# Grouped-query attention in a two-layer block: one more step between scores and transposes, with the dense products as a stage of their own

## The reference, cut to what matters

```python
qa, ka, va, za, qb, kb, vb, zb, ga, gb = split_cols(jnp.einsum('bld,de->ble', rms_norm_2(x, norm_g), w_in))
qa = apply_axial_rope(rms_norm_2(qa, q_norm_g), cos, sin)      # ka likewise
s = jnp.einsum('bqkgd,bskd->bkgqs', qb, k) * HEAD_DIM ** -0.5  # gqa_attention, 8 heads on 2 key heads
p = jax.nn.softmax(s, axis=-1)
oa = jnp.einsum('bkgqs,bskd->bqkgd', p, v) * jax.nn.silu(za)
```

## Time and profile before

| | |
|---|---|
| runs | 1706.32, 1709.43, 1713.77 us |
| profiled execution | 1706.15 us, span 1704.8 us, mean TensorE clock 0.982 |
| busy in the span | PE 1621.7 us (95%), DVE 872.2 (51%), ACT 620.7 (36%) |
| grouped attention of layer 0 | about 783.7 to 916 us of the span |
| grouped attention of layer 1 | about 1278 to 1422.5 us of the span |

### The profile page before, as it was taken

How to read it: one execution, slowest core, us unless ns; L and a number is a source line. 1 busy time by engine, 2 the same in 40 slices (tenths; PEclk the granted TensorE clock), 3 DMA queues, 4 the chain that set the end, 5 groups by cost and what they waited for, 6 DMA issues and landing times.

```text
span 1704.8 us, 24772 instructions
## 1 busy us (share of the span) xinstructions
PE 1621.7 (95%) x10349; PEld 1381.2 (81%) x10349; DVE 872.2 (51%) x1560; ACT 620.7 (36%) x1100; POOL 52.4 (3%) x52
## 2 busy tenths in 40 slices
PE   7999989999999999999999898999999998989997
PEld 5898767777888888899888777999988877667886
DVE  4434555556644655945554454346554455444543
ACT  5232244344322333723344342223233343433233
POOL 0000000000000000020000000000020000000000
PEclk9999989999999999999999899999999999999999
DMA  6234400014333322422111201224422112012331
GB/s 192 75 78 93 105 13 13 26 57 121 93 99 99 99 99 75 112 50 75 50 51 30 71 26 63 76 86 137 75 51 74 50 50 68 20 38 85 101 111 50
DMA packets 175599, 125.21 MB, mean 73 GB/s; under 512 B 48752, under 2 KB 172272, under 8 KB 175488
## 3 DMA queue, kind: packets, MB, share of 16 engines
q1 hardware_dynamic: 175488, 123.63, 25.4%
HBM read 121.52 MB, written 2.10 MB: 73 GB/s over the span
## 4 chain that ended last, share of the span: by engine, by line
PE 89%; DVE 4%; ACT 3%; issue 2%; POOL 0%; DVEq 0%; ACTq 0%; POOLq 0%
PE bank L576 69%; PE bank L2648 2%; PE bank L2680 2%; PE bank L2660 2%; PE bank L1581 2%; PE bank L3028 1%; PE bank L1540 1%; PE bank L2559 1%; PE bank L2991 1%; ACT w_hi L523 1%; PE bank L1467 1%; PE bank L1242 1%; PE bank L2510 1%; PE bank L3007 1%; ACT probs L1520 1%
## 5 line engine op out<-in xcount | busy, mean ns | idle before, releaser
L576 PE MATMUL bank<-h_hi,w_hi 128*128 128x512 f32 (+2 forms) x920 | 326.8, 375 | 9.4 <-issue 4.1
L532 DVE TENSOR_TENSOR w_lo<-w_raw,w_hi 128x2048 fp32r<-128x2048 f32 (+2 forms) x117 | 241.2, 2061 | 183.2 <-ACT w_hi L523 182.9
L576 PE MATMUL bank<-h_lo,w_hi 128*128 128x512 f32 (+2 forms) x920 | 322.4, 370 | 0.0
L576 PE MATMUL bank<-h_hi,w_lo 128*128 128x512 f32 (+2 forms) x920 | 320.9, 369 | 0.0
L523 ACT ACTIVATE w_hi<-w_raw 128x2048 fp32r<-128x2048 f32 (+2 forms) x117 | 201.1, 1720 | 67.0 <-DMA w_raw<-w_in 30.4
L576 PEld LDWEIGHTS bank<-h_hi,w_hi 128*128 128x128 f32 (+1 forms) x920 | 166.4, 189 | 53.0 <-issue 19.2
L576 PE MATMUL bank<-g_hi,w_hi 128*128 128x264 f32 (+1 forms) x784 | 197.8, 316 | 3.2 <-DVE g_lo L1693 1.8
L576 PE MATMUL bank<-g_lo,w_hi 128*128 128x264 f32 (+1 forms) x784 | 195.0, 312 | 0.0
L576 PE MATMUL bank<-g_hi,w_lo 128*128 128x264 f32 (+1 forms) x784 | 194.3, 311 | 0.0
L576 PEld LDWEIGHTS bank<-h_hi,w_lo 128*128 128x128 f32 (+1 forms) x920 | 166.5, 189 | 30.6
L576 PEld LDWEIGHTS bank<-h_lo,w_hi 128*128 128x128 f32 (+1 forms) x920 | 166.2, 189 | 29.5 <-issue 0.5
(11 more groups left out here) (561 smaller groups left out, 2578.4 us busy)
## 6 DMA issues: line engine op xcount, KB each, us to landing
w_raw<-w_in SPq DMA_DIRECT2D x45, 1024.0 KB, 5.3
w_raw<-w_up SPq DMA_DIRECT2D x32, 512.0 KB, 4.9
w_raw<-w_in SPq DMA_DIRECT2D x40, 256.0 KB, 4.5
w_raw<-w_down SPq DMA_DIRECT2D x8, 1024.0 KB, 5.1
w_raw<-w_out SPq DMA_DIRECT2D x8, 1024.0 KB, 5.1
w_raw<-w_out SPq DMA_DIRECT2D x8, 512.0 KB, 3.4
w_raw<-w_ple_gate SPq DMA_DIRECT2D x4, 1024.0 KB, 5.1
w_raw<-w_o_attn SPq DMA_DIRECT2D x8, 512.0 KB, 3.4
```

The lines of the kernel that those rows point to most:

```text
L532: DV.e.tensor_tensor(wlo[u % RING][:, 0:n], raw[u % RING][:, 0:n], whi[u % RING][:, 0:n].bitcast(F32), ALU.subtract).then_inc(*w_low(u))
L576: ins = PE.e.matmul(out, stationary[a](k), moving[b](k)[i], start=first and n == 0, stop=last and n == 2)
```

## The change

`filled` already has a parameter `apart`. With it, `pipeline` gets the stages score, give, turn, value, so that step s of the schedule is: score of item s, fill of item s - 1, turn of item s - 2, value of item s - 3. The change sets it in the three streams of the grouped attention, for both layers. No instruction is added or taken away, and no buffer or wait is edited.

```diff
@@ pe_gqa, L2686; the same line in ac_gqa, L2743, and dv_gqa, L2794
-            filled(items_g, first_steps(fill, fill_in_gqa(l)), fill_in_gqa(l), score, turn, value)
+            filled(items_g, first_steps(fill, fill_in_gqa(l)), fill_in_gqa(l), score, turn, value, apart=True)
```

## The result

The changed kernel takes 1726.73 us (median; 1723.47 to 1728.06), the kernel before 1708.87 us (1706.32 to 1713.77): a ratio of 1.0109, 95% interval 1.009 to 1.0128. It is slower by 17.9 us; 1727 was forecast. The profiled execution took 1726.40 us, its span is 1725.1 us.

What follows compares the result with a forecast made beforehand. PE, busy 95% of the span, was taken to bound the kernel; layer 0 +13.6, layer 1 +1.3 and clock +3.4 gave 18.3 us on 1706.15, 1724.5, or 1727 beside the median; range 1717 to 1738.

Steps and rivals of the forecast that it cites:

- the two bare starts: First step of each layer's stage, without a fill: the second score pair waits 2.86 us for item 1's exponentials.
- the za steps: Layer 0, steps 2 and 4: ACT's tanh and copy stand ahead of the second exponentials; 0.9 us each, 1.8 together.
- the tile ends: Layer 0, steps 10, 18, 26: DVE's closing copy stands ahead of the second maximum; 0.75, 0.75 and 1.7 us, together 3.2.
- steps 6, 8, 12, 14, 16, 20: Layer 0: chain from fill's end to next score pair, 2.76 us, outlasts PE's cover, 2.08; stalls 0.7, at 8 and 16 0.6.
- vb 22, 24, 28: Layer 0 fills of 24 instructions, evacuated by ACT at 22 and DVE at 24, 28: stalls 0.1, 0.4, 0.5 us.
- last value product but one: Layer 0, step 31: value 28, 29 waits some 0.9 us for DVE's last copy, behind exp 31 and meta exponentials.
- Rival B: Rival in the experiments: the new order costs PE itself something every period; +9 us for either layer alone; no chance given.
- The old waits: Layer 1 before: transposes behind the inverse multiplication, value products behind DVE's copy, score pairs behind exponentials; 5.5 us, to go.
- two low stretches: Behind each layer's 2.86 us start gap the clock runs at half for some 3.4 us, costing 1.7 each, +3.4 together.
- The rival in which the clock swings: Every stall of 0.6 us or more is followed by 3.4 us at 1.2 GHz: 31 us more, about 1758; chance 0.08.
- The chain fits in its cover: Score pair starts 2.08 us after the fill's end, so layer 0 stalls only at its start: +3.6, about 1713; chance 0.10.
- Faster: Removed waits count in full, starts are hidden and the clock holds: -5.5 us, 1704; chance 0.02.

## Why the prediction was right

**The order of the streams.** The step that the prediction starts from, DVE's second maximum queued behind the evacuation, is shown by the kernel with DVE's and ACT's order alone and by the one that takes DVE's back. It is not the whole loss. DVE's evacuation by itself was worth 3.9 us of layer 0's stage, and the two bare starts with their clock 8.4 us of the whole. That the za steps wait for the tanh and the tile ends for the closing copy is read from the order of the streams and its prices; neither was moved by itself. What is shown of them is that all waits of score pairs in layer 0 go with the fills in odd steps.

**The terms.** Waits in layer 0, forecast start to start, and the profile's brackets in the changed kernel:

| | forecast | measured |
|---|---|---|
| start | 2.86 | 2.79 |
| steps 2, 4 (za) | 0.9, 0.9 | 1.03, 0.67 |
| steps 6, 8, 12, 14, 16, 20 | 0.7, 0.6, 0.7, 0.7, 0.6, 0.7 | 0.58, 0.40, 0.51, 0.51, 0.40, 0.50 |
| tile ends 10, 18, 26 | 0.75, 0.75, 1.7 | 0.68, 0.68, 1.73 |
| vb 22, 24, 28 | 0.1, 0.4, 0.5 | 0, 0.25, 0.28 |
| last value product but one | 0.9 | 0.82 |

Each stands where it was put, and no other came. As idle time they are 11.7 us more than before (12.66 less 0.96), not 13.6; a part of the difference is the overlap that the brackets leave out. In a period with nothing special, as that of step 14, the chain is 2.71 us (857.05 to 859.76), and the cover is 0.53 + 1.03 + 0.59 = 2.15, not 2.08, since the turn behind a value product takes 0.59. The stall is 0.56, not 0.7.

**What was missing.** PE is busy 5.8 us longer in layer 0, and the clock takes 3.4 of it. The other 2.4 us comes in two parts.

The first is a cost of PE's own order, at which I had put nothing. In the kernel before a fill starts 0.41 us behind the start of a turn; in the changed one a score pair follows the turn instead, and the only such pair that shows no wait starts 0.59 us behind it:

```profile
897.08 0.66 PE L2660 MATMUL bank<-identity,gqa_probs_a 128*128 128x128 f32 x4
897.67 1.13 PE L2648 MATMUL bank<-k_a,q_a 64*128 64x512 f32 x4
```

The kernel whose fills stand in odd steps has the same 0.59 us between a turn and a value product, and its period without any wait takes 9.18 us (806.68 to 815.86), that of the kernel before 8.96:

```profile
815.86 1.13 PE L2648 MATMUL bank<-k_a,q_a 64*128 64x512 f32 x4
816.92 0.66 PE L2660 MATMUL bank<-identity,gqa_probs_a 128*128 128x128 f32 x4
817.51 1.09 PE L2680 MATMUL bank<-gqa_probsT_a,va_a 128*64 128x128 f32 x16
```

Over its whole layer 0 PE is busy 1.5 us longer than before. Its order is not quite that of the changed kernel, so 1.5 us is an estimate for the latter. Rival B of the experiments is thus true in a small part. What in PE makes the difference was not tried.

The second part, the 0.9 us that are left, is no further cost but the other side of the brackets: where PE waits, the turn ahead counts as busy for its full 0.66 us, where it does not, for 0.59. Start to start the stalls of layer 0 are therefore 11.7 + 0.9 = 12.6 us, where 13.6 were forecast, and PE's own order adds 1.5. Without the clock layer 0 lost 14.1 us: two errors, -1.0 and +1.5, that mostly cancelled.

**Layer 1.** Without its 1.7 us of clock the stage grew by 0.6 us; 1.3 were forecast. The start waited 2.79 us, and of the six periods all but that of step 22 stalled: 1.00 and 0.90 (za), 0.51, 0.51 and 0.17. The old waits went.

**The clock.** Forecast were two low stretches, 3.4 us. The changed kernel's profile has three, 5.1 us. Rows of PE at the start and at step 26 in layer 0, and the windows behind them; the third stands behind layer 1's start:

```profile
787.08 1.13 PE L2648 MATMUL bank<-k_a,q_a 64*128 64x512 f32 x4 [2.79 <-ACT gqa_probs_a L2721]
...
913.54 0.70 PE L2648 MATMUL bank<-k_a,q_a 64*128 64x512 f32 x2 [1.73 <-ACT gqa_probs_a L2721]
```

```profile
788.50:791.50 3.00, 3.00 (x17) 3.00 (x16) 1.27 (x3) 0.87 (x2) 0.00 (x0) 0.52 0.00 0
915.00:918.00 3.00, 3.00 (x16) 3.00 (x16) 0.61 (x2) 0.87 (x2) 0.00 (x0) 0.50 0.00 0
```

The one behind step 26 is the drop that the prediction named as open; the same gap in three of the experiments was not followed by one (see the last section). So this 1.7 us need not come in every execution. The rival in which the clock swings behind every small gap did not come: all other windows of the stages are at 1.00. So the Trainium skill's case in "TensorE: Matmul & The Clock Gate", section "A second HAM failure mode: psum-queue depth-cycling", is not this one: 20 gaps of 0.17 to 1.03 us in the changed kernel's stages left the clock alone.

In two places the prediction misread the gaps of the kernel before. Behind the gap ahead of 954.40 the clock was at 0.50 for 10.2 us and not for at most 8, so a drop can cost 5.1 us, over the bound of 4. And it left out a gap of 1.72 us ahead of 973.48, the one nearest to that of step 26, behind which the clock held:

```profile
953.10:963.30 10.20, 8.90 (x41) 7.71 (x42) 3.76 (x22) 5.21 (x21) 0.00 (x0) 0.50 0.07 25
973.00:977.00 4.00, 3.52 (x30) 2.29 (x30) 0.65 (x4) 3.01 (x11) 0.00 (x0) 1.00 0.01 2
```

**The sum.** 14.1 + 0.6 + 5.1 = 19.8 us for the two stages of the profiled executions (spans 20.3 apart), 18.3 forecast, and 17.9 between the medians. The near hit of 1727 on 1726.73 owes something to luck; the range of 1717 to 1738 is the fair claim.

**The rivals.** "The chain fits in its cover" fell with 2.71 against 2.1 us. "Faster" fell with it. That the deeper order can be had for 1.9 us, as 1709.43 us with fills in odd steps shows, I had not thought of, nor that the 5.5 us can be won without it.

## What to carry to other kernels

When one item's work is moved past another's in streams that run strictly in order, write out the new order of every engine, not of the busiest alone: here PE's order became more relaxed, and DVE's put a step that waits for the end of a long product in front of one that the next product needs. Place independent work so that it stands between the last step of a chain and its consumer, and never between the chain's own steps; a schedule by share (19 in 32) breaks that silently. A deeper pipeline also leaves its first step bare, and in all six bare starts of 2.79 us in these profiles the clock fell besides.

## What the runs showed that I had not expected

- A gap of 1.73 us ahead of 913.54 was followed by 3.4 us at 1.2 GHz in the changed kernel. The same gap at step 26 was not in the kernel with the new order in layer 0 alone, nor in those with DVE's late evacuation and the earlier first fill, nor was one of 1.74 us ahead of 1408.35 in the kernel with fills in odd steps; its clock over 1409 to 1412 is 1.00. A gap of 1.34 us ahead of 797.53, in the kernel with the earlier first fill, was followed by a low clock, though its twin in layer 1 and gaps of 1.34 to 1.72 us in the kernel before were not. At these lengths it can go either way.
- The low stretch need not be 3.4 us. In the kernel with the new order in layer 1 alone it lasted from about 1283.4 to 1290.3, behind the same start gap of 2.79 us, and cost 3.4 us rather than 1.7. Layer 0's start in the kernel with DVE's late evacuation did the same (792.0 to 798.9):

```profile
1284.00:1290.00 6.00, 5.67 (x13) 3.39 (x14) 1.51 (x3) 1.15 (x4) 0.00 (x0) 0.50 0.03 10
```

- Up to layer 0's stage, in unchanged code, executions differ by some 5 us in the clock alone. Added up from the granted clock of each half microsecond, the low stretches up to there cost 15.4 us in the profiles of the kernel before and the changed one, and 20.5 us in those of the kernels with DVE's and ACT's order alone and with DVE's late evacuation.
- What stands around a turn changes when the next product can start: a fill 0.41 us behind it, and a value product 0.59 us if a score pair stood ahead of the turn, 0.53 us if a fill did, all at the full clock.
